# A two-block transformer kernel on one core: attention blocks, mixer and launch issued in new orders

## The reference

```
# first block, DEPTH 2
layer 0: h += even_mixer(rmsnorm(h));  h += cross_attn(h, mem);  h += swiglu(h)
layer 1: h += conformer_conv(rmsnorm(h));  h += cross_attn(h, mem);  h += moe_swiglu(h)   # 8 experts, top 2
cross_attn: q = xn@wq; k, v = rmsnorm(mem)@wkv; 4 heads of 256; softmax(q k / 16) v; @ wo
# second block, DEPTH 2, the same x
h = rms_norm(x) @ w_in            # columns of five groups of 4 heads
mla, fox, moba, diff, mem = five kinds of attention, softmax over 256 keys
x = x + concat(five outputs) @ w_o
x = x + (silu(causal_dwconv(xn @ w_gate)) * (xn @ w_up)) @ w_down
```

## Time and profile before

| | before |
|---|---|
| median of 3 runs | 2312.94 us (2311.32 to 2318.18) |
| profiled execution | 2312.42 us, its span 2310.4 us |
| PE busy | 2281.7 us, 99% of the span |
| PEld busy | 2048.8 us, 89% |
| DVE busy | 1790.5 us, 77% |
| ACT busy | 1366.9 us, 59% |
| chain that ended last | PE 93%, DVE 5%, ACT 2% |

### The profile page before, as it was taken

The page is one execution under the profiler, slowest core; times in us unless marked ns, Lnnn a source line. Parts: engine busy times, 40 slices in busy tenths (PEclk is TensorE's granted clock), DMA queues, the critical chain, the costliest instruction groups (busy, mean ns, idle before and its releaser), DMA issues.

```text
span 2310.4 us, 33375 instructions
## 1 busy us (share of the span) xinstructions
PE 2281.7 (99%) x14316; PEld 2048.8 (89%) x14316; DVE 1790.5 (77%) x1840; ACT 1366.9 (59%) x1355; POOL 122.8 (5%) x94
## 2 busy tenths in 40 slices
PE   9999999999999999999999999999999999999999
PEld 8989999899988888888888888888889999889999
DVE  7856656766788989898889888987777676777765
ACT  5445434465577777777777777777555344645342
POOL 3001000001100000000000000000210001310000
PEclk9999999999999999999999999999999999999999
DMA  8644565463599999999999999995434655333553
GB/s 276 200 146 158 171 206 171 144 219 126 194 375 374 364 349 355 373 363 358 345 378 361 373 335 373 366 372 204 137 111 137 213 180 172 119 128 122 189 166 109
DMA packets 309786, 566.88 MB, mean 245 GB/s; under 512 B 12482, under 2 KB 137697, under 8 KB 309504
## 3 DMA queue, kind: packets, MB, share of 16 engines
q1 hardware_dynamic: 304848, 559.34, 69.2%
q10 hardware_dynamic: 4784, 5.35, 0.7%
HBM read 563.60 MB, written 1.05 MB: 244 GB/s over the span
## 4 chain that ended last, share of the span: by engine, by line
PE 93%; DVE 5%; ACT 2%; issue 0%; DMA 0%; ACTq 0%; SPq 0%; DVEq 0%
PE bank L1080 27%; PE bank L844 16%; PE bank L1098 13%; PE bank L684 9%; PE bank L828 7%; PE bank L672 7%; PE bank L257 4%; PE bank L696 2%; PE bank L1450 2%; PE bank L658 2%; DVE wL L206 1%; PE bank L1397 1%; DVE small L218 1%; ACT sq L232 1%; DVE ra L209 1%; DVE arena L206 1%
## 5 line engine op out<-in xcount | busy, mean ns | idle before, releaser
L206 DVE TENSOR_TENSOR wL<-raw,wH 128x2048 fp32r<-128x2048 f32 (+3 forms) x438 | 962.2, 2202 | 310.3 <-ACT wH L235 308.7
L235 ACT ACTIVATE wH<-raw 128x2048 fp32r<-128x2048 f32 (+3 forms) x438 | 799.9, 1831 | 383.3 <-PE bank L844 107.0
L1080 PE MATMUL bank<-wH,ra 128*128 128x512 f32 x1792 | 576.6, 393 | 0.1
L1080 PEld LDWEIGHTS bank<-wH,ra 128*128 128x128 f32 x1792 | 336.5, 188 | 69.9 <-DVE wL L206 1.6
L844 PE MATMUL bank<-ra,wH 128*128 128x256 f32 x2112 | 383.7, 284 | 2.7 <-DVE arena L227 2.7
L1080 PE MATMUL bank<-wL,ra 128*128 128x512 f32 x896 | 348.6, 389 | 0.0
L844 PEld LDWEIGHTS bank<-ra,wH 128*128 128x128 f32 x2112 | 330.6, 193 | 4.5 <-DVE arena L227 3.5
L844 PE MATMUL bank<-ra,wL 128*128 128x256 f32 x1056 | 299.5, 284 | 0.0
L1098 PE MATMUL bank<-wH,ra 128*128 128x512 f32 x896 | 285.3, 389 | 0.0
L206 DVE TENSOR_TENSOR wL<-arena,wH 128x2048 fp32r<-128x2048 f32 x112 | 256.3, 2288 | 1.5 <-ACT wH L235 1.4
L235 ACT ACTIVATE wH<-arena 128x2048 fp32r<-128x2048 f32 x112 | 215.1, 1920 | 61.0 <-PE bank L1080 61.0
(11 more groups left out here) (219 smaller groups left out, 2769.7 us busy)
## 6 DMA issues: line engine op xcount, KB each, us to landing
raw<-in_od_moe_gu SPq DMA_DIRECT2D x168, 1024.0 KB, 7.3
arena<-in_od_moe_gu SPq DMA_DIRECT2D x56, 1024.0 KB, 7.3
raw<-in_od_moe_down SPq DMA_DIRECT2D x56, 1024.0 KB, 6.8
arena<-in_od_moe_down SPq DMA_DIRECT2D x56, 1024.0 KB, 7.2
raw<-in_ev_ffn_gu SPq DMA_DIRECT2D x22, 1024.0 KB, 5.1
raw<-in_ffn_w_gate SPq DMA_DIRECT2D x22, 1024.0 KB, 5.5
raw<-in_ffn_w_up SPq DMA_DIRECT2D x22, 1024.0 KB, 5.4
raw<-in_ffn_w_down SPq DMA_DIRECT2D x22, 1024.0 KB, 5.0
```

The costliest lines, as they stand in the source:

```text
L206: self.op.tensor_tensor(out, a, b, op).then_inc(*self.sig.up(name))
L235: self.op.activation(out, a, ACT.Copy, **kw).then_inc(*self.sig.up(name))
L1080: m = p.op.matmul(out[:, :], a, b, start=half == 0 and c == 0 and i == 0, stop=half == 1 and c == 3 and i == 2)
```

## The change

No product, transpose or vector operation is added or taken out of the computation, apart from three more matmuls on zeros and one tiny ACT copy at launch. The order changes at these places:

- `cols` is loaded as 8 columns ahead of x and the rest behind it; ACT copies one element as soon as the constant is there (which brings its table load forward); nine matmuls on zeros instead of six.
- Mixer: the four `z4 copy` are done in a row, the splits behind them.
- Cross attention: each job waits for the query columns of its head alone; the first output transposes come after job 8, the last ones inside the first `wo` product, behind its first chunk (`last_turn`).
- `tail` follows every addition instead of every second; ACT's `act_x` waits per chunk.
- End of the experts: DVE makes the split of the block `in 0 mla 1` in the middle of the additions to `hT`, no longer ahead of the output's scaling.
- Second block: `turn(n)` comes behind the next half column product (n = 1 to 6); DVE's `rope_norm` of moba goes behind `top(7)`; `pe_out_turn` and some splits move.

```
 def pe_cross(self, p, l):
...
+        def last_turn(p):
+            span, p.span = p.span, (3, 8) if l else p.span
+            self.pe_to_fm(p, s, self.cross_o, 4, 8, 7)
+            p.span = span
...
+        self.pe_fm(p, ("wo", l), 2, 8, self.MEM, o_ready, lambda nb: (self.dve, ("wo", l, "res", nb)),
+                   {i + 1: lambda q, i=i: self.pe_route_in(q, i) for i in range(3)} if l else {}, None, {0: last_turn})
 def pe_second(self, p, l):
...
         value(0)
+        columns("moba_qk", 0, first)
         turn(1)
-        columns("moba_qk", 0, first)
         score(2)
...
+        columns("mem_q", 0, first)
+        turn(5)
+        score(6)
         if l == 0:
             self.pe_spread(p, "s0")
-        columns("moba_v", 1, other)
-        value(4)
-        turn(5)
-        columns("mem_q", 0, first)
-        score(6)
-        self.pe_out_turn(p, s, "fox", 3)
         columns("mem_q", 0, other)
         value(5)
+        columns("mem_q", 1, first)
         turn(6)
-        columns("mem_q", 1, first)
         score(7)
         columns("mem_q", 1, other)
-        self.pe_qk_turn(p, s, l, "moba")
         value(6)
         turn(7)
+        self.pe_qk_turn(p, s, l, "moba")
...
-        product("fox", 8, 12)
+        product("fox", 8, 16)
         self.pe_out_turn(p, s, "diff", 7)
-        product("fox", 12, 16)
...
         product("diff", 8, 12)
+        self.pe_out_turn(p, s, "moba", 9)
         score(11)
         product("diff", 12, 16)
-        self.pe_out_turn(p, s, "moba", 9)
 def act_mixer(self, a):
-        a.wait_ge(*got["cols"].of("cols"))
+        a.wait_ge(*self.dve.of("eps"))
+        a.cp("table", self.stat[:, 0, 0:1], self.epst[:, 0:1])
+        a.wait_ge(*got["gain"].of("gain"))
 def dve_moe(self, v):
-                self.dve_blocks(v, ("moe", pe_, pf, "down", 1))
+                if q <= last:
+                    self.dve_blocks(v, ("moe", pe_, pf, "down", 1))
 def dve_second(self, v, l):
+            if l == 0 and c == 5:
+                blocks("moe", NE - 1, NRD - 1, "down", 1)
...
-        self.dve_rope_norm(v, s, l, "moba", 64, 1)
         value(5)
         turned(6)
         top(7)
+        self.dve_rope_norm(v, s, l, "moba", 64, 1)
+        columns("mem_q")
+        value(6)
+        turned(7)
+        self.dve_turned(v, s, l, "moba")
         blocks("in", l, "mem_q", 1)
...
-        blocks("w_o", l, "fox")
+        final_norm(4)
         self.dve_out_turned(v, s, "diff")
         value(8)
         turned(9)
+        blocks("w_o", l, "fox")
         top(10)
 def cross_jobs(self, l):
-                 (self.dve, ("v", l, 1, 1)), (self.dve, ("wq", l, "copy", 7))]
+                 (self.dve, ("v", l, 1, 1))]
...
+        jobs.hook(pe=lambda p: self.pe_to_fm(p, s, self.cross_o, 0, 4, 3),
+                  act=lambda a: self.act_to_fm(a, s, self.MEM, 0, 4), dve=lambda v: None)
+        jobs.late = lambda v: self.dve_to_fm(v, s, self.MEM, 0, 4)
```

More of the change, by code:

```diff
@@ L306, in __init__ @@
         self.more_in = [signal(f"more_in{i}", 16) for i in range(2)]
-        self.got = {n: signal(f"{n}_in", 16) for n in ("x0", "x1", "x2", "x3", *(f"w{j}" for j in range(12)), "cst", "cols", "inv", "mem", "rows", "pos", "router",
+        self.got = {n: signal(f"{n}_in", 16) for n in ("x0", "x1", "x2", "x3", *(f"w{j}" for j in range(12)), "cst", "gain", "cols", "inv", "mem", "rows", "pos", "router",
                                                        "mem2_0", "mem2_1", "gate_b", "conv_b")}
@@ L568, in sync_program @@
         got = self.got
-        s.op.dma_start(self.cols[:, :], d["cols"]).then_inc(*got["cols"].up("cols"))
+        s.op.dma_start(self.cols[:, 0:C], d["cols"][:, 0:C]).then_inc(*got["gain"].up("gain"))
         for j in range(4):
@@ L707, in pe_warm @@
         p.wait_ge(*self.dve.of("no_mask"))
-        for i in range(6):
-            p.op.matmul(self.banks[7][:, 0:256], self.zeros[:, 0:128], self.zeros[:, :], start=i == 0, stop=i == 5)
+        for i in range(9):
+            p.op.matmul(self.banks[7][:, 0:256], self.zeros[:, 0:128], self.zeros[:, :], start=i == 0, stop=i == 8)
     def pe_mixer(self, p):
@@ L1249, in pe_second @@
         value(1)
+        columns("moba_qk", 1, first)
         turn(2)
-        columns("moba_qk", 1, first)
         score(3)
@@ L1255, in pe_second @@
         value(2)
+        columns("moba_v", 0, first)
         turn(3)
-        columns("moba_v", 0, first)
         score(4)
@@ L1479, in tensor_program, with act_x @@
         self.pe_outside(p)
-    def act_x(self, a, s, gain, g0, j, dst):
+    def act_x(self, a, s, gain, g0, j, dst, have=None):
         for c in (2 * j, 2 * j + 1):
+            if have:
+                a.wait_ge(*have(c))
             a.cp((s, "hi", c), dst[0][:, c, :], self.hT[:, c, :], scale=self.col(gain, g0 + c))
@@ L1491, in act_x_all @@
         for j in range(4):
-            for c in (2 * j, 2 * j + 1):
-                a.wait_ge(*have(c))
-            self.act_x(a, s, gain, g0, j, dst)
+            self.act_x(a, s, gain, g0, j, dst, have)
     def act_total(self, a, s, *free):
@@ L1539, in act_mixer @@
             self.act_first(a, 2, j)
+        a.wait_ge(*got["cols"].of("cols"))
         self.act_next = 3
@@ L2085, in act_second @@
         exp(5)
+        columns("moba_v")
+        self.act_out_turned(a, s, "fox")
+        blocks("in", l, "mem_q", 0)
+        exp(6)
         if l == 0:
@@ L2211, in dve_mixer @@
     def dve_mixer(self, v):
-        v.wait_ge(*self.got["cols"].of("cols"))
+        v.wait_ge(*self.got["gain"].of("gain"))
         for i in range(3):
@@ L2219, in dve_mixer @@
             self.dve.mark(("w_lo", i))
+        v.wait_ge(*self.got["cols"].of("cols"))
         self.dve_next = 3
@@ L2266, in dve_mixer @@
         v.own()
-        for n in range(2):
-            self.dve_blocks(v, ("z4", n))
-            for nb in (2 * n, 2 * n + 1):
-                v.wait_ge(*self.pe.of(("z4", nb)))
-                v.tt(("z4", "copy", nb), self.y[:, nb, :], self.y[:, nb, :], self.ps(("z4", nb))[:, 0:256], ALU.mult)
+        self.dve_blocks(v, ("z4", 0))
+        for nb in range(4):
+            v.wait_ge(*self.pe.of(("z4", nb)))
+            v.tt(("z4", "copy", nb), self.y[:, nb, :], self.y[:, nb, :], self.ps(("z4", nb))[:, 0:256], ALU.mult)
         for k in (0, 1):
             self.dve_y_lo(v, k)
+        self.dve_blocks(v, ("z4", 1))
         self.dve_blocks(v, ("w_out", 0))
+        self.dve_blocks(v, ("w_out", 1))
         self.dve_norm(v, "mem0", self.memT, "xa_norm_mem", 0, self.inv_m, self.MEM)
@@ L2361, in dve_attend @@
                 j["done"](v, (s, "o", n), j["out"], self.ps((s, "value", n))[:, 0:j["dv"]], self.stat[:, n % 16, 3:4])
+            if i == len(jobs.all):
+                jobs.late(v)
     def out_scaled(self, v, name, dst, ps, rinv):
@@ L3190, in dve_second @@
         blocks("in", l, "fox_v", 1)
+        turned(0)
+        blocks("in", l, "diff_v", 0)
+        top(1)
         self.dve_mean_heads(v, s, "diff", sqh[:, :], 32)
-        blocks("in", l, "diff_v", 0)
-        turned(0)
-        top(1)
-        blocks("in", l, "diff_v", 1)
         columns("diff_v")
@@ L3231, in dve_second @@
         v.tt((s, "n", "mem_k"), k4, k4, self.heads("mem_k").broadcast_to([128, 2, 4, 64]), ALU.mult)
-        columns("mem_q")
-        self.dve_turned(v, s, l, "moba")
-        value(6)
-        turned(7)
         top(8)
```

39 lines of the change are left out of this document (15 added, 24 removed).

## The result

The changed kernel took 2291.72 us (median of 4 runs, 2290.34 to 2293.62) beside 2313.9 of the kernel before: a ratio of 0.9905, 95% interval 0.9889 to 0.992. In the experiments' five rounds it took 2295.10 (2290.96 to 2297.92) beside 2312.53: 0.9925, interval 0.9912 to 0.9939. Both lie in the range of the forecast (2289 to 2303), whose number was 2294.4. The second series is wider than the first; experiments 9 to 11 say what is known of that.

A forecast was written before the change was run, and what follows sets the result against it. PE was taken as the bound, busy 2281.7 of 2310.4 us. Terms 11.6 + 2.9 + 1.6 + 0.3 + 0.6 - 0.8 = 16.2, with 1.8 together 18.0, took 2312.4 to 2294.4; range 2289 to 2303.

The forecast's parts named there:

- drain term: Whole kernel: each removed PE wait is worth 0.16 us more, 0 to 3.5 at some 22 waits; 1.8 taken.
- Turns, score 7, diff and moba: Second block's attention, both layers: waits of 11.1 go, full clock behind score 7 gives 3.0; 11.6 us after new waits.
- Minus 2.0: Second block, moba's transposes: a new wait of 1.0 us a layer, as DVE needs 5.5 and PE has 4.5.
- Minus 0.5: Second block, first layer: a split ahead of top(10) makes the maximum late and turn 10 waits 0.5 us.
- 0.2 left of 0.6: Cross attention: of the last output transposes' wait of 0.6 us, 0.2 stays; the whole term gains 2.9.
- Mixer: Mixer: the waits of 1.08 at 65.56 and 0.55 at 80.77 go; gain 1.6 us.
- Launch: Launch: table load of 1.28 us leaves the path, but 18 rows of matmuls on zeros delay PE; gain 0.6.
- Experts' end: End of the experts: the moved split makes the last two additions 1.0 us later; loss 0.8 replacing a wait of 1.3.
- The waits move on: Rival, second block's attention: the turned map's copy delays the exponential and waits reappear; 2301 us, chance 0.17.
- The clock falls again: Second rival: the new wait at moba's transposes makes PE's clock fall; 2298 to 2300 us, chance 0.13.
- Nothing measurable: Rival, whole kernel: PE's waits reflect a slower feed, loads above all, and return at the next block; 2306 to 2313, chance 0.06.
- The slower case: Rival, loop of 12 quads: the turned map's copy ahead of every maximum makes DVE the pace; 2325 us, chance 0.03.

The follow-up runs named there:

- experiments 9 to 11: Changed kernel with reordered experts' end and second block, 2288.63 us; changed kernel again, 2295.10; changed kernel with last cross attention output transposes back, 2299.02.
- b_pair: Kernel before with only moba's rope_norm behind the maximum of quad 7 and moba's transposes behind turn 7; 2312.92 us.
- a_cross: Changed kernel with the last four output transposes of each cross attention ahead of the wo product again; 2299.02 us.
- b_second: Kernel before with the change's edits in the second block's attention alone, without the split between the additions; 2302.85 us.
- a_table: Changed kernel without ACT's copy of one element, so its table load comes behind x again; 2294.08 us.
- a_warm6: Changed kernel with six matmuls on zeros at launch instead of nine, table load still early; 2293.74 us.
- b_warm9: Kernel before with nine matmuls on zeros at launch instead of six, nothing else; 2314.90 us.
- a_experts: Changed kernel with the split at the experts' end ahead of the output's scaling again, not between the additions; 2289.39 us.
- b_turns: Kernel before with only turns 1 to 6 moved on PE behind the next half column product; 2308.47 us.
- the version with the fewest waits: Changed kernel with early squares and low part 4 at the experts' end, later moba transposes and reordered splits around quad 10; 2288.63 us.
- a_ kind: Kernels that are the changed kernel with one part undone or altered; no single time.
- after_again: The changed kernel once more, nothing altered, in five rounds beside the kernel before; 2295.10 us.

## Why the prediction was right, and where it was not

The forecast, not a rival, came true: 19.3 us in the profile against 18.0, 2291.7 and 2295.1 us against 2294.4. The mechanism was right: PE's small waits went where the order said, and the time with them. That the number is this near is in part luck. The stretches other than the taps and the experts' end gained 4.7 more than forecast, of which the drain term was to cover 1.8, and the taps, of which the forecast had nothing, took 1.5 back. Without that the profile would have shown some 20.8.

- **Turns, score 7, diff and moba.** The removed waits measured 11.1, as said, and b_pair shows that the wait of score 7 and its half clock go together. "Minus 2.0" for moba's transposes was 1.0 and a remnant of 0.4 at turn 7: DVE needed 5.1 from the start of the maximum to the end of value(6), the row at 1690.92, and not 5.5, and PE reached the second half of the transposes at 1691.22, 5.0 behind the start of its half product, and not 4.5. "Minus 0.5" for turn 10 was 0.4, but in both layers; the prediction named only the first, although the split moved in both. Together 2.2 lost instead of 2.5.
- **Drain term.** I took half of 3.5. In the attention 11.1 + 3.0 - 2.2 = 11.9, but 13.26 were measured: 1.4 over, for 14 waits less 6 new ones 0.17 each. In the cross attention it is 1.06 for 6 waits, 0.18 each. In the mixer it is 0.52 for 2. The whole 0.16 a wait is paid, and a little more, for some 16 waits net and not 22: 2.9 in place of 1.8, the term of the sum that was mis-sized most. It works the other way too: at the experts' end the listed waits grew by 0.27 only (0.37, 0.18, 0.39 and 0.59 for 1.26), and the loss of 0.88 comes with four waits in place of one. The conformer start is the exception, 0.39 for a wait of 0.52.
- **Cross attention.** "0.2 left of 0.6" did not happen: six matmuls cover the last transposes even behind two low parts. a_cross shows that the wait without them would be 0.67.
- **Mixer.** 2.57 for 1.6: the two waits gave 2.15 with their drains, and 0.43 more came between 27 and 39 us, where PE before had short stalls of 0.1 to 0.2 that the view of waits does not list. b_second, with before's mixer and launch, takes 84.46 there, as before did; but a_table, which has the changed mixer, keeps just these stalls. So the 0.43 is the table load's, and belongs to the launch.
- **Launch.** 1.06 against 0.6 between these two profiles, but this is the term whose reasoning failed. I priced the table load against slow matmuls on zeros. a_table and a_warm6 show that neither alone costs anything visible up to the first sum; in a_warm6 the second pair of chunks sets the pace. What the late table load cost alone, in the one run that has it alone, is the 0.43 behind it. What counts more is the half clock that the earlier trace rows happened not to have: over five profiles with before's late table load (b_warm9 among them) the sum of squares starts at 25.20, 26.67, 27.19, 27.44 and 27.52, over seven with the changed one at 24.13 to 24.75. Between the middle values, 27.19 and 24.24, lie 2.95 us.
- **Experts' end.** The loss of 0.8 was 0.88, and a_experts gave back 0.89. Its place was half right: the wait for the squares is 0.59, and the rest stands at the low part of chunk 4, which I had not followed. What I did not see is that the clock can fall there, as in a_cross, a version of my second rival at a place where it had no price.
- **The rivals.** "The waits move on" was shown at work in b_turns (1.6 of 4.0), and the change escapes it only since it mends score 7 as well. "The clock falls again" happened at the experts' end in a_cross and for longer than before at the taps in after, not at moba's transposes. Its reading that the trace shows the fall behind 2.0 left out that the same trace has whole clock behind the launch gap of 2.22. "Nothing measurable" falls with b_second. The slower case was far off: the largest new wait is 0.59.

## What to carry to other kernels

On an engine that is 99% busy, the waits in its view can be summed almost as they stand, with some 0.17 us more for each that goes and less for each that comes (0.17, 0.18 and 0.26 in three places here, and none at a fourth), provided that the next place that asks for the same late engine is mended in the same step. Put a long split where the engine would wait anyway, and then look at what the split has pushed behind it, on the other engines as well: at the experts' end two reordered small operations were worth 1.25, and turned a move that lost 0.88 into one that gains 0.37. And judge a new small wait by what PE's clock does behind it, over several runs: the version with the fewest waits was also the one with the narrowest spread, though four runs do not show that the one brings the other.

## What the runs showed of the hardware

PE's granted clock was at half (1.2 GHz) in four places: at launch, behind score 7, at the experts' end, and at the taps. At score 7 it fell in all six layers that waited 2.0 or 2.8, and in none of the 22 whose wait was gone. The taps are the odd one. PE shows no gap there at all, only eight matmuls that use 31 of 128 partitions, and yet seven of 14 profiles have half clock in their course or behind them. Why it is these seven is open. The stretch from the taps to the conformer's first product then took 61.57 us (five profiles of the a_ kind, whole clock), 63.06 (three) or 64.58 (after): steps of 1.5. The same step stands between the two first layers that waited 2.0 at score 7, 120.75 and 122.33, and the 6.4 of a_cross is about four of them. So a fall cost 1.5 or about a multiple here, and one and the same kernel pays it or not: after had 64.58, after_again 61.57. These are some 3 us that a single pair of profiles cannot compare.

The Trainium skill (TensorE: Matmul & The Clock Gate, Part 1) calls the throttled state the default, which activity releases, and says that the count of slow matmuls varies between runs of one kernel. The traces agree on both. The rows of the matmuls on zeros start 0.43 apart at first and, in most profiles, 0.22 apart later, and twelve of them took 5.49 us in after and 4.96 in after_again, which are one kernel (4.38 to 5.49 over all). In before the pace of 0.43 holds to the twelfth, though the view of the granted clock has whole clock there. The taps add that the clock also fell where PE's rows show no idle time.
